# Scoring keys by queries in an attention and recurrence block, with row maxima from a product of their own, one head ahead

## The chip, the cores and the metric

The kernel runs on one core of a Trainium2 chip. The metric is device time in microseconds (us), the median of the runs. A core has five engines with queues of their own: PE (TensorE, matrix products), DVE (VectorE), ACT (ScalarE), POOL (GpSimd) and SP (SyncE, here it only issues transfers). They meet through semaphores: an instruction waits until a count is reached. PE reads its operands from SBUF (128 partitions) and writes to PSUM (8 banks of 512 fp32 columns). A product has a stationary operand, which is loaded first (PEld in the profile), and a moving one, which is streamed through.

## The reference

One transformer block on 1024 tokens of width 1024, fp32. An input projection feeds two mixers, which are joined by an output projection and followed by an MLP. The change lies in the first mixer:

```python
def block_fn(blk):                      # 128 queries of every head
    s = einsum(qb, kc) * scale          # 63 compressed keys
    p_cmp = masked_softmax(s, cmp_end <= t)
    o_cmp = einsum(p_cmp, vc)
    ...
    s = einsum(qb, k_sel) * scale       # 16 of 16 blocks: all keys up to t
    p = masked_softmax(s, pos <= t)
    o_slc = einsum(p, v_sel)
    ...
    s = einsum(qb, kwb) * scale         # the last 512 keys
    p = masked_softmax(s, wmask)
    o_win = einsum(p, vwb)
    return g0 * o_cmp + g1 * o_slc + g2 * o_win
```

There are 8 query heads of 64 dimensions and 2 groups of keys. As 16 blocks of 64 keys are all there are, the selection selects every block, and the second branch is plain causal attention.

## The kernel before

The stages follow one another: norm and transposes of the input, the projection in blocks of 512 columns (the compression of keys and values lies between two of them), the transposed keys, the attention of the first mixer, the recurrence of the second, the output projection, and the MLP. Each projection multiplies fp32 numbers as three products of a high and a low half (type fp32r).

The attention is a loop of four passages over two heads each. A passage has a list of 34 items. For a head there is one item for the compressed keys of all 1024 queries, and for each of the 8 tiles of 128 queries one over all keys so far ("slc", 1 to 8 key tiles) and one over the window ("win", 1 to 5 tiles): 66 key tiles in all, 36 and 30. Queries lie in PSUM partitions, keys along the columns. An item goes through these steps:

- PE (L1374) multiplies the stationary queries by the keys' high half and by their low half. `q_stack` holds the 64 dimensions twice, high half above, low half below, so that two products give nearly fp32. A product of identity and mask (L1379) adds the causal mask. An item has at least 256 columns and is cut in two banks over 512.
- DVE (L1058) takes the negative row maximum, and ACT (L835) writes exp(score − maximum) to `probs` with its row sum (an ACTIVATION_READ_ACCUMULATOR stands behind it).
- PE (L1389) transposes each 128x128 tile of `probs` into bank 4 or 5, and ACT (L849) or DVE (L1116) copies it to `probs_T`.
- PE (L1414) multiplies the stationary `probs_T` by the values (64 columns), in fp32: each such product stands in the trace as two MATMULs.
- DVE (L1087 to L1096) multiplies by the gates and the inverse sums and adds the result to `nsa`.

The compressed keys go the same way with a mask product (L1354), eight fp32 products of 64 columns (L1358), L1062, L1064, L826 and L1408. PE's order is written out by hand: transposes of item j, scores of item j+3, outputs of item j−1. The queries of the next heads are transposed at items 9 and 27 (L568; POOL copies them to `stage`, L665; ACT and DVE split them, L818, L1051). Ahead of the loop stand the same steps for the keys and for the first queries (L568, L805, L1035, L809, L1040), and behind it SP, POOL and ACT wait for the last output (`o_free`) before the recurrence begins.

## Time and profile before

| | |
|---|---|
| median of 3 runs | 1743.29 us (1740.09 to 1744.35) |
| profiled execution, first to last instruction | 1735.6 us |
| attention, from the transposes of the first queries to the last output | 364.2 to 698.2 us |
| PE busy over the whole span | 1573.1 us (91%) |
| DVE, ACT, POOL busy | 712.8 (41%), 443.6 (26%), 509.6 (29%) us |

Busy shares of PE are shares of recorded time: matrix products overlap in their records, so the step from one start to the next is the better measure of what one costs. The granted clock of TensorE is 1.0 where it runs at 2.4 GHz and 0.50 at 1.2 GHz.

### The profile page before, as it was taken

How to read it: one execution, taken by the hardware profiler on the slowest of the kernel's cores; microseconds unless marked ns; L12 is line 12 of the kernel's file. 1: busy time of each engine (PE TensorE's matmuls, PEld its weight loads, DVE VectorE, ACT ScalarE, POOL GpSimd, SP SyncE). 2: the span in 40 equal slices, each digit the busy share in tenths (PEclk: the TensorE clock that was granted, in tenths of full speed). 3: DMA queues.
4: the chain of work that ended last, by engine and by line, in shares of the span. 5: the costliest groups of instructions: out<-in, count | busy, mean ns of one | idle time of the engine just before them, and what ended most of it. 6: DMA issues, size and time to landing. Idle time of an engine off the chain costs nothing. (4 is left out here: it accounts for less than half of the span.)

```text
span 1735.6 us, 24765 instructions
## 1 busy us (share of the span) xinstructions
PE 1573.1 (91%) x8345; PEld 1328.8 (77%) x8345; DVE 712.8 (41%) x1311; ACT 443.6 (26%) x1007; POOL 509.6 (29%) x505
## 2 busy tenths in 40 slices
PE   3999999989999999467659989999999999999998
PEld 2988877878888888366548768888888888888886
DVE  5003830046576666899961143222222222222222
ACT  5014120144445455533361122020202020202020
POOL 1433322310000000665613313333333333333331
PEclk9999999979899999788979979999999999999999
DMA  4211131000000000100031101111111111111112
GB/s 143 62 48 49 37 97 32 17 6 2 0 0 0 0 0 0 45 0 0 0 121 46 60 16 49 49 48 48 47 48 44 48 48 48 48 48 43 53 43 97
DMA packets 36484, 69.09 MB, mean 40 GB/s; under 512 B 5688, under 2 KB 7264, under 8 KB 36448
## 3 DMA queue, kind: packets, MB, share of 16 engines
q1 hardware_dynamic: 34176, 67.78, 12.7%
q10 hardware_dynamic: 2272, 0.84, 0.2%
q8 instruction: 21, 0.34, 0.1%
q14 instruction: 15, 0.12, 0.0%
HBM read 64.41 MB, written 4.19 MB: 40 GB/s over the span
## 5 line engine op out<-in xcount | busy, mean ns | idle before, releaser
L427 POOL CAST w_high<-w_raw 128x512 fp32r<-128x512 f32 (+1 forms) x200 | 129.4, 647 | 767.8 <-issue 383.2
L429 POOL TENSOR_TENSOR w_low<-w_raw,w_high 128x512 fp32r<-128x512 f32 (+1 forms) x200 | 261.2, 1306 | 16.1
L435 PE MATMUL ps<-hT_high,w_high 128*128 128x512 f32 x640 | 249.8, 390 | 1.9 <-DVE hT_low L494 1.9
L435 PE MATMUL ps<-hT_low,w_high 128*128 128x512 f32 x640 | 249.5, 390 | 0.0
L435 PE MATMUL ps<-hT_high,w_low 128*128 128x512 f32 x640 | 249.4, 390 | 0.0
L1207 DVE TENSOR_TENSOR x<-ps,x 128x512 f32<-128x512 f32 x144 | 98.1, 692 | 285.8 <-PE ps L435 285.8
L435 PE MATMUL ps<-w_high,hidden_high 128*128 128x512 f32 x512 | 202.0, 394 | 2.0 <-ACT relu L932 1.9
L435 PE MATMUL ps<-w_high,hidden_low 128*128 128x512 f32 x512 | 199.4, 389 | 0.0
L435 PE MATMUL ps<-w_low,hidden_high 128*128 128x512 f32 x512 | 199.3, 389 | 0.0
L1240 DVE TENSOR_TENSOR relu_squared<-relu 128x512 f32<-128x512 f32 x64 | 57.1, 902 | 312.5 <-ACT relu L932 312.5
L932 ACT ACTIVATE relu<-ps 128x512 f32<-128x512 f32 x64 | 37.6, 588 | 574.4 <-PE ps L435 573.7
L435 PE MATMUL ps<-w_high,hT_high 128*128 128x512 f32 (+1 forms) x448 | 168.9, 377 | 4.1 <-DVE hT_low L494 3.1
L435 PE MATMUL ps<-w_low,hT_high 128*128 128x512 f32 (+1 forms) x448 | 168.8, 377 | 0.0
L435 PE MATMUL ps<-w_high,hT_low 128*128 128x512 f32 (+1 forms) x448 | 168.5, 376 | 0.0
L435 PEld LDWEIGHTS ps<-hT_high,w_high 128*128 128x128 f32 x640 | 120.5, 188 | 27.1 <-issue 2.1
L435 PEld LDWEIGHTS ps<-hT_high,w_low 128*128 128x128 f32 x640 | 120.5, 188 | 25.2
L435 PEld LDWEIGHTS ps<-hT_low,w_high 128*128 128x128 f32 x640 | 120.5, 188 | 25.1
L1414 PE MATMUL ps<-nsa,probs_T 128*128 x1056 | 138.3, 275 | 0.0
L1439 PE MATMUL ps<-hgrn_kq 128*128 128x128 f32 x448 | 77.3, 334 | 58.1 <-DVE hgrn_kq L1166 57.2
L1414 PEld LDWEIGHTS ps<-nsa,probs_T 128*128 128x128 f32 x1056 | 129.6, 194 | 0.0
L435 PEld LDWEIGHTS ps<-w_high,hidden_high 128*128 128x128 f32 x512 | 96.1, 188 | 31.2 <-ACT relu L932 8.9
L1439 PEld LDWEIGHTS ps<-hgrn_kq 128*128 128x128 f32 x448 | 68.5, 238 | 66.9 <-DVE hgrn_kq L1166 51.0
(179 smaller groups left out, 2356.3 us busy)
## 6 DMA issues: line engine op xcount, KB each, us to landing
w_raw<-in_w_mlp_in_dram SPq DMA_DIRECT2D x64, 256.0 KB, 2.7
w_raw<-in_w_mlp_out_dram SPq DMA_DIRECT2D x64, 256.0 KB, 2.7
w_raw<-in_w_in_dram SPq DMA_DIRECT2D x48, 256.0 KB, 2.7
x_in<-in_x_dram SPq DMA_DIRECT2D x8, 512.0 KB, 8.7
w_raw<-in_w_out_dram SPq DMA_DIRECT2D x16, 256.0 KB, 4.0
x<-in_x_dram SPq DMA_DIRECT2D x8, 512.0 KB, 7.6
out_dram<-x SPq DMA_DIRECT2D x8, 512.0 KB, 4.7
w_raw<-in_w_in_dram SPq DMA_DIRECT2D x8, 140.0 KB, 7.2
```

The costliest lines, as they stand in the source:

```text
L427: eng.tensor_copy(w_high[:, s, 0:width], w_raw[:, s, 0:width]).then_inc(w_highs, 1)
L429: eng.tensor_tensor(w_low[:, s, 0:width], w_raw[:, s, 0:width], w_high[:, s, 0:width].bitcast(F32), ALU.subtract).then_inc(w_split, 1)
L435: ins = nc.tensor.matmul(out_ap, a_hl[i], b_hl[j], start=first and n == 0, stop=last and n == 2)
L932: act.activation(relu[:, b % 4, :], ps[:, b, :], ACT.Relu).then_inc(m1_out, 1)
L1207: dve.tensor_tensor(xs, ps[:, t, :], xs, ALU.add).then_inc(res_out, 1)
L1240: dve.tensor_tensor(relu2[:, b % 4, :], relu[:, b % 4, :], relu[:, b % 4, :], ALU.mult).then_inc(sqd, 1)
L1414: ins = nc.tensor.matmul(ps[:, O_BANK + it.pair(j) % 2, c:c + DK], lhs, nsa[:, tiles[n], bass.ds(g * DK + v0, DK)], start=n == 0, stop=n = ...
L1439: ins = nc.tensor.matmul(ps[:, A_BANKS[u % len(A_BANKS)], h * P:(h + 1) * P], lhs(h), rhs(h), start=True, stop=True)
```

## The change

It leaves the stages around the attention as they are and writes the attention anew, without a loop over passages.

- Scores are made with keys in the partitions and queries in the columns (`scores_T`, L1330, L1331). The stationary operand is a tile of keys, the moving one up to 512 queries. The exponential of it is already `probs_T`, so the transposes of the probabilities and the copies of them are gone.
- The row maximum can't be subtracted by ACT's bias any more, since it runs along the columns. It becomes a further row of the contraction: the second key operand `k_low_and_ones` holds the low half of the keys in rows 0 to 63 and a row of ones at 64, 65 or 66 (one for each branch); the second query operand `q_and_max` holds the queries and, in these three rows, the negative maxima. It comes from a transpose of `q_max_stage`, in which POOL puts the queries and DVE the maxima.
- The maxima come from a product of their own (`scores_for_max`, L1299 to L1309), of the high half of the keys only, in the layout of before. There are 25 pieces of up to 512 columns for a head: one for the compressed keys and 24 of 1 to 4 key tiles. DVE takes the negative maximum of each (L1038, L1042) and joins those of queries 512 to 1023 from two parts (L1048). The pieces of head h+1 are made while head h is scored, two in each of the places 3 to 15.
- A head has 19 units of 512 columns (the last has 256), 6 for the first half of the queries and 13 for the second. In each place PE makes one unit's scores, then transposes or pieces for the next head, then the outputs of a unit two places back (up to four back at the start of a half, when outputs of three units come together in one place).
- The values get a column of ones (`v_and_ones`, 65 columns), so that the output product gives the row sums too; ACT's row sums are gone.
- The outputs of half a head fill two banks, and DVE empties them in four operations (`finalize`): reciprocal of 12 sums, times the gates, 768 products, and the sum of the three branches (L1057, L1059, L1063, L1067). The last two signal `o_free` and `y_done`.
- All compressed keys are fp32r now, as a high and a low half (`cmp_k_high`, `cmp_k_low_and_ones`); a key past the end takes the place of a masked row's sum, and the table `valid` is gone.

The core of the diff:

```diff
+EARLY = 9
+P_SLOTS = 6
+S_BANK, ST_BANK, T_BANK, O_BANK = 0, 2, 4, 6
+QT_AT, MAX_AT, Q2_AT = 0, 3, (9, 17)
...
+            def scores_for_max(h, c):
+                br, t, k0, k1, part = CHUNKS[c]
+                g, C = h // HPG, NM * h + c
+                if c == 0:
+                    pe.wait_ge(t_dve, q_low(h, 1))
+                if C >= 2:
+                    pe.wait_ge(max_done, C - 1)
...
+                ins = nc.tensor.matmul(o[:, 0:(k1 - k0) * P], QT[:, h % 2, t * P:(t + 1) * P], KS_H[:, br - 1, g, k0 * P:k1 * P],
+                                       start=True, stop=not tiles, skip_group_check=True)
...
+            def scores_T(h, u):
+                g, U = h // HPG, NU * h + u
+                if UNITS[u]["place"] == 0:
+                    pe.wait_ge(t_act, m_index(h, UNITS[u]["half"]) + 1)
+                if U >= 2:
+                    pe.wait_ge(exp_done, U - 1)
...
+                    nc.tensor.matmul(o, k1, QT[:, h % 2, qs], start=True, stop=False, skip_group_check=True)
+                    ins = nc.tensor.matmul(o, k2, Q2[:, h % 2, qs], start=False, stop=not tiles, skip_group_check=True)
...
+            for c in range(NM):
+                scores_for_max(0, c)
+            for half in range(2):
+                q_max(0, half)
...
+            for h in range(NH):
+                for u in range(NU):
+                    scores_T(h, u)
+                    if h + 1 < NH:
+                        if u in (QT_AT, QT_AT + 1):
+                            q_stack(h + 1, u - QT_AT)
+                        for c in range(2 * (u - MAX_AT), min(2 * (u - MAX_AT) + 2, NM)):
+                            if c >= 0:
+                                scores_for_max(h + 1, c)
+                        if u in Q2_AT:
+                            q_max(h + 1, Q2_AT.index(u))
+                    for h2, u2 in OUT_AT.get(NU * h + u, []):
+                        outputs(h2, u2)
```

And on DVE:

```diff
+            def finalize(h, half):
...
+                dve.wait_ge(pv_done, NU * h + [u for u, x in enumerate(UNITS) if x["half"] == half][-1] + 1)
+                o = out_view()
+                rec, cf = coef[:, 0, :, :], coef[:, 1, :, :]
+                at_.mark(dve.reciprocal(rec.rearrange("p (b t) r -> p b (t r)", b=2).unsqueeze(3), o[:, :, :, DK:OV]))
...
+            for h in range(NH):
+                for u in range(NU):
+                    if h + 1 < NH:
+                        if u in (QT_AT, QT_AT + 1):
+                            low_T(h + 1, u - QT_AT)
+                        for c in range(2 * (u - MAX_AT), min(2 * (u - MAX_AT) + 2, NM)):
+                            if c >= 0:
+                                maximum(h + 1, c)
+                    for h2, u2 in OUT_AT.get(NU * h + u, []):
+                        if UNITS[u2]["ends"]:
+                            finalize(h2, UNITS[u2]["half"])
```

How the instructions stand in a row shows it best at three places. First PE in the middle of a head. Before, an item of four key tiles: two transposes of the probabilities (of the item three back), two score products of 512 columns, a mask, two outputs.

```order
L1389 MATMUL ps<-eye,probs 128x128 [waits t_bank_emptied_by_act,exp_done]
L1389 MATMUL ps<-eye,probs 128x128
L1374 MATMUL ps<-k_high,q_stack 128x512
L1374 MATMUL ps<-k_low,q_stack 128x512
L1379 MATMUL ps<-masks 128x128
L1402 REGISTER_ALU
L1414 MATMUL ps<-nsa,probs_T 128x64 [waits t_bank_emptied_by_dve]
```

After, PE in places 8 and 9 of a head: the scores of a unit, two pieces for the maxima of the next head, again a unit and two pieces, and the transposes with the first half's maxima.

```order
L1330 MATMUL ps<-q_stack,k_high 128x512 [waits exp_done]
L1331 MATMUL ps<-q_and_max,k_low_and_ones 128x512
L1306 MATMUL ps<-k_high,q_stack 128x128 [waits max_done]
L1309 MATMUL ps<-masks 128x128
L1306 MATMUL ps<-k_high,q_stack 128x384 [waits max_done]
L1309 MATMUL ps<-masks 128x128
L1330 MATMUL ps<-q_stack,k_high 128x512 [waits exp_done]
L1331 MATMUL ps<-q_and_max,k_low_and_ones 128x512
L1306 MATMUL ps<-k_high,q_stack 128x256 [waits max_done]
L1309 MATMUL ps<-masks 128x128
L1306 MATMUL ps<-k_high,q_stack 128x512 [waits max_done]
L566 MATMUL ps<-eye,q_max_stage 128x128 [waits t_bank_emptied_by_dve,max_in_stage,q_max_stage_ready]
```

The transposes of the probabilities are gone, and every second product now waits for a maximum that DVE has taken two pieces earlier.

On DVE, before, in the middle of a passage: one maximum, one copy of transposed probabilities, and a short group for the outputs of one item alternate.

```order
L1058 TENSOR_REDUCE negmax<-ps 128x1 [waits qk_done]
L1113 REGISTER_ALU
L1116 COPY probs_T<-ps 128x512 [waits pv_done,t_full]
L1087 RECIPROCAL coef<-row_sums 128x2 [waits exp_done]
L105 REGISTER_ALU
L1089 ISA [waits att_step]
L1089 TENSOR_TENSOR coef<-coef,gates 128x2
```

After, DVE over one head: the compressed keys' maximum and nine more, the outputs of the first half of the queries, the fifteen other maxima, the joining of the parts, the low halves of the next queries, and the outputs of the second half.

```order
L1038 TENSOR_REDUCE q_max_stage<-ps 128x8 [waits t_full,scores_for_max_full]
L1042 TENSOR_REDUCE q_max_stage<-ps 128x1 [waits scores_for_max_full] x8
L1042 TENSOR_REDUCE part_max<-ps 128x1 [waits max_done,scores_for_max_full]
L1057 RECIPROCAL coef<-ps 128x12 [waits pv_done]
L1059 TENSOR_TENSOR coef<-coef,gates 128x12 [waits att_step]
L1063 TENSOR_TENSOR weighted_outputs<-ps,coef 128x768 [waits y_done,att_step]
L1067 TENSOR_REDUCE nsa<-weighted_outputs 128x4x64 [waits o_free]
L1042 TENSOR_REDUCE part_max<-ps 128x1 [waits scores_for_max_full] x15
L1048 TENSOR_TENSOR q_max_stage<-part_max 128x4x2 [waits max_done]
L1028 TENSOR_TENSOR q_stack<-ps,q_stack 64x512 [waits t_bank_emptied_by_act] x2
L1057 RECIPROCAL coef<-ps 128x12 [waits pv_done]
L1059 TENSOR_TENSOR coef<-coef,gates 128x12 [waits att_step]
```

The outputs now come in two long groups, and the maxima of pieces 10 to 24 stand behind the first of them.

Third, PE ahead of the first head. Before, the transposes of the first queries were followed by the scores of three items and then by the steady order. After, all 25 pieces of the first head come first (here the first and the last of them), then the transposes with the maxima, then the first unit.

```order
L1299 MATMUL ps<-cmask,masks 128x512 [waits t_bank_emptied_by_dve,cmp_k_low_ready,masks_loaded]
L1301 MATMUL ps<-cmp_k_high,q_stack 128x64 x8
L1306 MATMUL ps<-k_high,q_stack 128x128
L1309 MATMUL ps<-masks 128x128
```

```order
L1306 MATMUL ps<-k_high,q_stack 128x256 [waits max_done]
L1309 MATMUL ps<-masks 128x128
L566 MATMUL ps<-eye,q_max_stage 128x128 [waits t_bank_emptied_by_dve,max_in_stage,q_max_stage_ready]
L566 MATMUL ps<-eye,q_max_stage 128x128 x3
L566 MATMUL ps<-eye,q_max_stage 128x128 [waits t_bank_emptied_by_dve,max_in_stage,q_max_stage_ready]
L566 MATMUL ps<-eye,q_max_stage 128x128 x3
L1330 MATMUL ps<-q_stack,cmp_k_high 128x512 [waits v_and_ones_ready,t_bank_emptied_by_act,ones_rows_ready,t_bank_emptied_by_dve]
```

What moved is the whole maximum work of one head: it now lies between the first queries and the first unit.

## Rows read from the trace of the kernel before

**Rows 1.** The page: busy time of each engine (share) xinstructions, then 40 slices.

```profile
PE 1573.1 (91%) x8345; PEld 1328.8 (77%) x8345; DVE 712.8 (41%) x1311; ACT 443.6 (26%) x1007; POOL 509.6 (29%) x505
...
PE   3999999989999999467659989999999999999998
```

**Rows 2.** Windows over the attention: stretch, length, busy time of each engine, clock.

```profile
361.50:381.90 20.40, 17.08 (x76) 15.25 (x76) 8.44 (x17) 7.74 (x20) 2.29 (x3) 0.50 0.01 1
381.90:457.00 75.10, 71.23 (x587) 64.20 (x585) 50.80 (x123) 37.44 (x93) 2.03 (x2) 1.00 0.01 1
457.00:467.30 10.30, 9.89 (x44) 8.66 (x44) 4.57 (x12) 4.11 (x16) 0.00 (x0) 0.50 0.00 0
```

**Rows 3.** Windows over the second and the third passage of two heads.

```profile
457.40:541.30 83.90, 79.79 (x623) 72.15 (x623) 54.40 (x131) 40.96 (x106) 2.03 (x2) 0.94 0.00 0
541.30:621.50 80.20, 75.87 (x622) 68.21 (x622) 53.86 (x131) 40.77 (x105) 2.03 (x2) 1.00 0.00 0
```

**Rows 4.** PE's waits in the third passage: total us, times, longest.

```profile
PE ps L1389 <- DVE q_stack L1051: 2.0, 2, 1.0
PE ps L1389 <- ACT probs L826: 1.7, 1, 1.7
PE ps L1374 <- ACT probs L835: 0.6, 2, 0.4
```

**Rows 5.** Timeline of PE, third passage: start us, us, instruction (320-column products, outputs, transposes).

```profile
562.34 0.83 PE L1389 MATMUL ps<-eye,probs 128*128 128x128 f32 x6
562.92 0.39 PE L1374 MATMUL ps<-k_high,q_stack 128*128 x1
563.15 0.31 PE L1374 MATMUL ps<-k_low,q_stack 128*128 x1
563.30 0.23 PE L1379 MATMUL ps<-masks 128*128 128x128 bf16 x1
563.34 0.39 PE L1374 MATMUL ps<-k_high,q_stack 128*128 x1
563.57 0.31 PE L1374 MATMUL ps<-k_low,q_stack 128*128 x1
563.72 0.23 PE L1379 MATMUL ps<-masks 128*128 128x128 bf16 x1
563.79 1.28 PE L1414 MATMUL ps<-nsa,probs_T 128*128 x10
```

**Rows 6.** Timeline: products of 512 columns, the start of a passage (256 columns), and compressed keys.

```profile
585.90 0.40 PE L1374 MATMUL ps<-k_low,q_stack 128*128 x1
586.14 0.23 PE L1379 MATMUL ps<-masks 128*128 128x128 bf16 x1
...
616.99 0.38 PE L1354 MATMUL ps<-cmask,masks 128*128 128x512 bf16 x1
617.20 1.90 PE L1358 MATMUL ps<-cmp_k,q_stack 128*128 x16
...
622.12 0.28 PE L1374 MATMUL ps<-k_low,q_stack 128*128 x1
622.25 0.23 PE L1379 MATMUL ps<-masks 128*128 128x128 bf16 x1
```

**Rows 7.** Groups of the third passage: line, operation, count | busy us, mean ns.

```profile
L1058 DVE TENSOR_REDUCE negmax<-ps 128x1 f32<-128x512 f32 x4 | 2.6, 681 | 0.0
L1051 DVE TENSOR_TENSOR q_stack<-ps,q_stack 64x512 fp32r<-64x512 f32 x4 | 2.6, 691 | 4.2 <-ACT q_stack L818 4.2
L1058 DVE TENSOR_REDUCE negmax<-ps 128x1 f32<-128x384 f32 x4 | 2.2, 553 | 0.3 <-PE ps L1379 0.3
L818 ACT ACTIVATE q_stack<-ps 128x512 fp32r<-128x512 f32 x4 | 2.2, 595 | 1.3 <-PE ps L568 1.3
L1058 DVE TENSOR_REDUCE negmax<-ps 128x1 f32<-128x768 f32 x2 | 1.9, 953 | 0.0
L1058 DVE TENSOR_REDUCE negmax<-ps 128x1 f32<-128x256 f32 x4 | 1.7, 420 | 0.5 <-PE ps L1379 0.5
L1062 DVE TENSOR_REDUCE cmp_max<-ps 128x8 f32<-128x512 f32 x2 | 1.4, 692 | 1.4 <-PE ps L1358 1.4
L1058 DVE TENSOR_REDUCE negmax<-ps 128x1 f32<-128x128 f32 x4 | 1.1, 284 | 0.1
L1075 DVE RECIPROCAL cmp_max<-cmp_max 128x8 f32<-128x8 f32 x2 | 0.4, 193 | 0.0
```

**Rows 8.** Timeline of the start: the first queries, and PE's first products.

```profile
364.22 1.94 PE L568 MATMUL ps<-eye,stage 128*128 128x128 f32 x8 [0.65 <-DVE k_low L1035]
...
366.83 0.69 DVE L1040 TENSOR_TENSOR q_stack<-ps,q_stack 64x512 fp32r<-64x512 f32 x1 [0.16 <-ACT q_stack L809]
...
367.58 0.61 PE L1354 MATMUL ps<-cmask,masks 128*128 128x512 bf16 x1 [1.42 <-DVE q_stack L1040]
367.66 3.64 PEld L1358 LDWEIGHTS ps<-cmp_k,q_stack 128*128 128x128 f32 x16
367.98 3.52 PE L1358 MATMUL ps<-cmp_k,q_stack 128*128 x16
```

**Rows 9.** Timeline of the end: the last outputs on DVE, and ACT's next step.

```profile
697.60 0.28 DVE L1094 SCALAR_TENSOR_TENSOR nsa<-ps,coef,nsa 128x64 f32 x1 [2.42 <-PE ps L1414]
697.92 0.28 DVE L1096 SCALAR_TENSOR_TENSOR nsa<-ps,coef,nsa 128x64 f32 x1
...
698.24 3.90 ACT L861 ACTIVATE hgrn_logf<-hgrn_qf 128x1024 f32<-128x1024 f32 x4 [1.69 <-DVE nsa L1096]
```

**Rows 10.** Timeline of the step from the compressed keys to the projection that follows.

```profile
264.65 0.57 ACT L796 ACTIVATE cmp_v<-ps 64x128 f32<-64x128 f32 x2 [1.39 <-PE ps L1283]
```

**Rows 11.** A group of POOL over 500 to 1000 us: the costliest form of its kind.

```profile
L690 POOL TENSOR_SCALAR hgrn_k<-hgrn_qf 128x1024 f32<-128x1024 f32 x4 | 8.0, 2029 | 0.0
```

More of the change, by code:

```diff
@@ L193, with window, score_units @@
-PREP_AT = 9
-NEXT_AT = 27
-FIRST = 10
-PT_SLOTS = 10
-P_SLOTS = 4
-AHEAD = 3
-S_BANKS = 4
-T_BANK = 4
-O_BANK = 6
+CMP, SLC, WIN = 0, 1, 2
+def window(t):
+    return max(0, t - WIN_T), t + 1
+def score_units():
+    units = []
+    for half in range(2):
+        t0 = 4 * half
+        whole, parts = [], []
+        for br in (SLC, WIN):
+            for kt in range(t0 + 4):
+                qs = [t for t in range(t0, t0 + 4) if (kt <= t if br == SLC else window(t)[0] <= kt <= t)]
+                (whole if len(qs) == 4 else parts).append((br, kt, qs[0], len(qs)))
+        mine = [[(CMP, 0, t0, 4)]] + [[c] for c in whole]
+        while parts:
+            a = max(parts, key=lambda c: c[3])
+            parts.remove(a)
+            b = next((c for c in parts if c[3] + a[3] == 4), None)
+            if b:
+                parts.remove(b)
+            mine.append([a, b] if b else [a])
+        for place, chunks in enumerate(mine):
+            units.append(dict(half=half, place=place, chunks=chunks, ends=place == len(mine) - 1,
+                              width=sum(c[3] for c in chunks) * P))
+    return units
@@ L202, with out_slots @@
+OV = DK + 1
+def out_slots():
+    when = {}
+    for h in range(NH):
+        for u, unit in enumerate(UNITS):
+            at = NU * h + u + 2 + max(0, 2 - unit["place"])
+            when.setdefault(at, []).append((h, u))
+    return when
+OUT_AT = out_slots()
 D_SLOTS, E_SLOTS, X_SLOTS = 4, 3, 4
@@ L1123, in _, with low_T @@
[L1123 to L1127 removed]
+            at_ = Steps(att_step)
+            def low_T(h, half):
+                T = q_index(h, half)
+                dve.wait_ge(t_act, T + 1)
+                q = QT[DK:P, h % 2, half * BW:(half + 1) * BW]
+                dve.tensor_tensor(q, ps[DK:P, T_BANK + T % 2, :], q.bitcast(F32), ALU.subtract).then_inc(t_dve, 1)
@@ new lines, in _ @@
+            for half in range(2):
+                low_T(0, half)
+            for c in range(NM):
+                maximum(0, c)
+            for h in range(NH):
+                for u in range(NU):
[8 more added lines that the diff above has]
+                            finalize(h2, UNITS[u2]["half"])
@@ new lines, in outputs @@
+            def outputs(h, u):
+                g, U, unit = h // HPG, NU * h + u, UNITS[u]
+                if unit["place"] == 0:
+                    pe.wait_ge(o_free, 2 * h + unit["half"])
+                pe.wait_ge(exp_done, U + 1)
+                col = 0
+                for br, kt, q0, nq in unit["chunks"]:
+                    for q in range(q0, q0 + nq):
+                        tt = q - 4 * unit["half"]
+                        m = 3 * (tt % 2) + br
+                        v = V1c[:, g, :] if br == CMP else V1[:, br - 1, g, kt, :]
+                        ins = nc.tensor.matmul(ps[:, O_BANK + tt // 2, m * OV:(m + 1) * OV], PT[:, U % P_SLOTS, col:col + P], v,
+                                               start=br == CMP and tt % 2 == 0, stop=unit["ends"], skip_group_check=True)
+                        col += P
+                ins.then_inc(pv_done, 1)
@@ L1435, in _ @@
+            for at in sorted(OUT_AT):
+                if at >= NU * NH:
+                    for h2, u2 in OUT_AT[at]:
+                        outputs(h2, u2)
+            pe.wait_ge(o_free, 2 * NH)
             pe.wait_ge(bc_done, 4)
```

555 lines of the change are left out of this document (202 added, 353 removed).

## The prediction

> **What bounds the kernel now.** I read the page first: PE is busy 91% of the span, and its digit is 8 or 9 all through the attention (slices 9 to 16) [rows 1]. Then the windows over the attention: in a passage of two heads PE is busy 75.87 of 80.2 us, DVE 53.86, ACT 40.77, POOL 2.03 [rows 3]. So PE sets this stage, and what the change does to DVE and ACT counts only where PE waits for them. PE's waits in a passage are 2.0, 1.7 and 0.6 us [rows 4], 4.3 in 80.2. Last the clock. The stage begins at 0.50 and is at 1.00 from 381.9; a second stretch at 0.50 lies at 457.0 to 467.3, just behind the change from the first passage to the second, and makes that passage 83.9 instead of 80.2 us, 3.7 more [rows 2, 3]. From the transposes of the first queries at 364.2 to the last output at 698.2 the stage takes 334.0 us [rows 8, 9].
>
> **What a PE instruction costs.** The step from a start to the next, all at clock 1.00. A product of 320 columns 0.15 us (563.57 to 563.72) [rows 5], of 512 0.24, of 256 0.13 [rows 6], so 384 about 0.18 and 448 0.20. A mask 0.07 (563.72 to 563.79), and 0.05 more where an fp32r product follows it: product, product, mask, product's step is 0.42 (562.92 to 563.34) against 2 x 0.15 + 0.07 [rows 5]. Ten fp32 outputs take 1.28, the last one 0.275 of it in the pipeline: 0.112 each, two for a tile whatever its width. Six transposes in 0.83: 0.111 each [rows 5]. The wide mask 0.21 (616.99 to 617.20), and 16 for the compressed keys 0.112 each [rows 6].
>
> As a test, one head of before: products 20 x 0.15 + 8 x 0.13 + 8 x 0.18 + 4 x 0.20 + 8 x 0.24 = 8.2; masks 1.6; compressed scores 0.21 + 16 x 0.112 = 2.0; outputs 148 x 0.112 = 16.6; transposes (66 + 4 + 8) x 0.11 = 8.6. Sum 37.0. The trace has 40.1 for a head, of which 2.2 are the waits of rows 4 and 0.9 shorter ones.
>
> **One head after.** Removed: 70 transposes of probabilities, 7.7 us, and the fp32 compressed scores, 2.0. Unchanged: 148 outputs, 16.6. They have 65 columns instead of 64, and their step was the same 0.112 at 64 columns [rows 5] as a transpose of 128 has. Added or changed:
> - Products, both kinds together: 29 of 512 columns x 0.235, 17 of 384 x 0.18, 17 of 256 x 0.13, 13 of 128. The last are not in the trace; no fp32r product there has under 256 columns. Below they are bounded by one loading of weights, the 0.112 of an output's step, above by an fp32 product, two records, 0.224 [rows 5]. I take 0.112, since 256 columns at 0.13 are already close to it. Sum 6.8 + 3.1 + 2.2 + 1.5 = 13.5.
> - 40 masks x 0.07 and 30 x 0.05 behind them: 4.3 (before 1.6). Three wide masks 0.7. Eight short products on the compressed keys 0.9.
> - 16 transposes, 8 of the queries and 8 with the maxima: 1.8.
>
> Sum 37.7 us, 0.7 more than before. The transposes that go are paid back by the second pass over the scores (7.2 for the maxima: 4.2 of products, 1.9 of masks, 1.1 of compressed keys) and by masks that are now made twice.
>
> DVE and ACT get much less. DVE has for a head 25 reductions: 0.69 + 5 x 0.284, 0.42 and 0.553 by their widths, 0.681 for 512 [rows 7], 13.1 together, two low halves 1.4, and two groups of outputs; ACT 19 exponentials at about 0.6, as a 512-column copy from PSUM has 0.595 [rows 7], and four copies. That is about 20 and 14 us in 41, so neither becomes the bound by its sum.
>
> **Where PE waits after.** A group of outputs on DVE is a reciprocal 0.19, a product with gates about as much, 768 columns from PSUM about 0.95 (a reduction of 768 has 0.953), and a sum of 768, again 0.95 [rows 7]: with the gaps 2.6 us. Behind it stand the next maxima, and PE, in order, may be only two pieces ahead of them.
> - Places 7 to 9. The group starts 0.25 after the outputs of place 7. The maximum of piece 10 (0.284) is ready at 0.25 + 2.6 + 0.28 + 0.18 for the signal = 3.3. PE has up to piece 12 only two units and two pieces: 0.47 + 0.42 + 0.47 = 1.4. It waits 2.0 there, and 0.4 more at piece 13. Behind PE's wait stand the transposes with the maxima and the outputs of place 10.
> - Places 1 to 4. The low half of the next queries comes first: unit 1's exponential ends about 3.4 us into the head, ACT's copy takes 0.6, DVE 0.69 [rows 7], which makes 4.8. Then the group of the second half, 2.6, and the compressed keys' maximum, 0.69: ready at 8.2. PE gets to piece 2, which needs it, at 7.0. It waits 1.2, and 0.3 around it.
>
> Together 3.9 us for a head against the 3.1 of before. A head takes 41.6, before 40.1. Were DVE's group hidden, nothing else would be late: the exponentials are asked for two places later, about 4 us against 0.9.
>
> **The start.** All 25 maxima of the first head lie ahead of the first unit. The queries are ready 3.3 us after 364.2, as before [rows 8]. Then wide mask and eight products at clock 0.50, 0.43 + 8 x 0.22, with the handover 2.4; then the reductions. DVE needs 13.1, and PE at 0.50 as much for a piece as DVE (512 columns and mask 0.43 + 0.11 + 0.2 of loading, against 0.681), so that a part of the handovers shows: 17.8, between 13.1 and 25 x 0.74. Then the joining, four transposes and the signal: 1.0. First unit 24.5 us after 364.2. POOL's new work (ones rows, two operations of 2048 columns at twice the 2.03 of 1024 [rows 11], and values) ends about 12 us after 364.2 and is hidden under this; if the maxima took under 10 us it would show.
>
> **The end.** The last head makes no maxima and no queries: 37.7 − 7.2 − 1.8 = 28.7, and 0.9 of waits. Then a whole group of outputs, 2.7, where before DVE had two small operations left, 697.60 to 698.20 [rows 9].
>
> **The sum.** 24.5 + 7 x 41.6 + 29.6 + 2.7 = 348.0. I add one stretch at half clock as before, 3.7, since waits of this length stand at the passages' ends now too [rows 2, 3]: 351.7, against 334.0. Before, the slow clock at the start (to 381.9) fell on real work, about 8 us; now it falls on a time that DVE sets anyway, which is in the sum. The compression stage gives 0.3 back, one copy of 0.28 instead of two [rows 10]. Span 1735.6 + 17.7 − 0.3 = 1753; the median stands 7.7 above the profiled span, so **1761 us**, 1.0% slower.
>
> **The rivals.**
> - *Short products are dear.* If an fp32r product of 128 columns costs what an fp32 one does, 0.224, that is 13 x 0.112 and something at the 64-column ones, 1.5 to 1.9 us for a head. A part falls into waits that are there anyway, so I count 8 to 12 in all: 1771. For it: nothing in the trace runs below 256 columns in fp32r. Against it: the step at 256 shows no floor but the loading. The Trainium skill, FP8 and Floating Point Precision, section TensorE Precision Notes, says that true FP32 takes four passes and a reduced FP32 is read and truncated, with no word on a least width; by that the cheap case holds, and the trace agrees as far as its 256-column rows at 0.13 go.
> - *More half clock.* Each head now has a wait of 2.0 and one of 1.2. If a stretch like 457.0 to 467.3 came in every second head, three more would cost 11: 1772. For it: the one of before lies where two passages meet and PE waits [rows 2]. Against it: the third passage has a wait of 1.7 too and stays at 1.00 [rows 3, 4].
> - *Faster: PE never waits for the maxima.* The place is DVE's group in places 7 and 1. If it takes under 1.1 us, a third of what the rows give, piece 12 is never late. Then a head takes 37.7 to 38, 8 x 3.7 less, and with the clock steady 3.7 less again: 1761 − 30 − 4 = 1727. The rows of 0.69 for 512 columns speak against it.
> - *No difference.* Half of the waits hidden (slots filled in another way than I think) and no stretch at half clock: 1761 − 15 − 4 = 1742, within the bound.
>
> **How the numbers follow.** About 0.3% (5 us) is what a measurement of this kernel can tell from no change. Forecast 1761 with its own spread of 1750 to 1768: 0.45. Short products dear: 0.25. More half clock: 0.12, both slower. No difference: 0.10. Faster: 0.08. So slower 0.82, same 0.10, faster 0.08. The range leaves out the faster case and the ends where two slow cases meet: 1745 to 1779.
>
> **What would show each step.** PE's busy time in the attention stays about what it was and its outputs' step stays 0.112; in it DVE falls by about a quarter and ACT by a third. The first unit stands near 388.7. From a head's first unit to the next are 41 to 42 us, with two waits for maxima (L1306 on DVE L1042 and L1038) of 1 to 2.5 us each. L1331 at 128 columns shows a step of 0.11 or 0.22. I am wrong if a head takes under 40 us, if ones rows or values from POOL hold the first unit, or if ACT holds PE at every unit.

## The result, and the profile after

The changed kernel takes 1758.12 us, median of 4 runs (1751.31 to 1760.86), beside 1741.69 us for the kernel before in the same comparison (4 runs, 1737.9 to 1744.35). The ratio is 1.0084, with an interval of 1.0061 to 1.0106: slower by 16 us, and inside the range. Where single executions of a kernel below stand over 1.5% above its fastest, they are given apart and no comparison uses them.

| | before | after |
|---|---|---|
| profiled span, us | 1735.6 | 1749.5 |
| median of all runs in this comparison, us | 1741.69 | 1758.12 |
| attention, from 364.2 to DVE's last step on the outputs, us | 334.0 | 348.0 |
| first unit or score after 364.2, us | 3.4 | 23.4 |

The page of after, as [rows 1]: busy time of each engine (share) xinstructions, then 40 slices of TensorE (PE) and its granted clock.

```profile
PE 1582.6 (90%) x8160; PEld 1317.0 (75%) x8177; DVE 642.7 (37%) x1078; ACT 384.0 (22%) x774; POOL 521.2 (30%) x521
...
PE   3999999979999999466759969999999999999998
...
PEclk8999999979998999788879979999999999999999
```

DVE and ACT are relieved by 70 and 60 us, PE does 9.5 us more. The windows of after, as [rows 2, 3]: stretch, length, busy time of PE, PEld, DVE, ACT and POOL with the number of instructions, clock (the last two numbers are the transfers' share and rate). They are the start, the passage of the first head, that of the second, that of the fifth, and of the fifth again its first wait and the stretch at 0.50.

```profile
364.00:387.60 23.60, 19.39 (x69) 12.80 (x70) 14.59 (x29) 1.68 (x3) 8.37 (x10) 0.57 0.00 1
387.60:427.50 39.90, 37.74 (x279) 31.41 (x280) 16.16 (x32) 14.84 (x26) 2.27 (x3) 0.98 0.00 1
427.50:468.10 40.60, 38.15 (x291) 32.33 (x292) 18.46 (x36) 13.09 (x23) 1.66 (x2) 1.00 0.01 1
549.50:596.20 46.70, 45.75 (x291) 38.23 (x292) 18.64 (x36) 13.09 (x23) 1.66 (x2) 0.82 0.00 1
...
556.30:557.20 0.90, 0.18 (x2) 0.04 (x1) 0.90 (x3) 0.60 (x1) 0.00 (x0) 1.00 0.00 0
...
559.60:576.60 17.00, 16.93 (x65) 13.18 (x64) 6.65 (x12) 2.81 (x5) 0.00 (x0) 0.50 0.00 0
```

From a head's first unit to the next head's are 39.90, 40.65, 40.66, 40.65, 46.79, 42.24 and 40.65 us. At the full clock a head takes 40.65: 38.15 us of PE's work and two waits. The fifth takes 6.1 more, because 17.0 us of it run at 0.50; the sixth has 3.4 us at 0.50. PE's waits in the second head, as [rows 4]: total us, times, longest. Behind them the same two waits on PE's timeline, and the first of the two DVE groups that make them.

```profile
PE ps L1306 <- DVE part_max L1042: 1.6, 1, 1.6
PE ps L1306 <- DVE q_max_stage L1038: 0.8, 1, 0.8
```

```profile
434.28 0.23 PE L1336 MATMUL ps<-masks 128*128 128x128 bf16 x1
435.33 0.33 PE L1306 MATMUL ps<-k_high,q_stack 128*128 128x128 f32 x1 [0.81 <-DVE q_max_stage L1038]
...
446.15 0.40 PE L1331 MATMUL ps<-q_and_max,k_low_and_ones 128*128 128x512 f32 x1
448.12 0.39 PE L1306 MATMUL ps<-k_high,q_stack 128*128 128x256 f32 x1 [1.57 <-DVE part_max L1042]
```

```profile
432.18 0.23 DVE L1057 RECIPROCAL coef<-ps 128x12 f32<-128x12 f32 x1
432.44 0.17 DVE L1059 TENSOR_TENSOR coef<-coef,gates 128x12 f32<-128x12 f32 x1
432.65 0.96 DVE L1063 TENSOR_TENSOR weighted_outputs<-ps,coef 128x768 f32<-128x768 f32 x1
433.64 1.03 DVE L1067 TENSOR_REDUCE nsa<-weighted_outputs 128x256 f32<-128x768 f32 x1
434.59 0.68 DVE L1038 TENSOR_REDUCE q_max_stage<-ps 128x8 f32<-128x512 f32 x1
```

PE has written two pieces for the maximum and needs one of their banks back. DVE is in the group of outputs from 432.18 to about 434.6 and takes the compressed keys' maximum only then; PE goes on at 435.33. The second wait is the same with the other half: there DVE's group holds up the maximum of a later piece (L1042).

The end, as [rows 9]: a whole group of 2.5 us lies behind the last outputs.

```profile
709.75 0.23 DVE L1057 RECIPROCAL coef<-ps 128x12 f32<-128x12 f32 x1 [15.75 <-PE ps L1353]
710.02 0.17 DVE L1059 TENSOR_TENSOR coef<-coef,gates 128x12 f32<-128x12 f32 x1
710.22 0.96 DVE L1063 TENSOR_TENSOR weighted_outputs<-ps,coef 128x768 f32<-128x768 f32 x1
711.22 1.03 DVE L1067 TENSOR_REDUCE nsa<-weighted_outputs 128x256 f32<-128x768 f32 x1
```

So the account of the attention is: 23.4 start, 39.9 + 6 x 40.65 = 283.8 for seven heads at the full clock, 7.7 for the half clock, 30.6 for the last head, 2.5 for the end. That is 348.0, and 14.0 more than before: the difference of the two spans is 13.9.

### The profile page after: what moved, and what is told of

It is laid out like the page before. It is cut to its first block and busy times, and to the rows that moved or that the text cites. A ratio compares the mean times of both kernels' runs of the same rounds, so it can differ in the third digit from the quotient of the medians.

```text
span 1749.5 us, 22153 instructions
## 1 busy us (share of the span) xinstructions
PE 1582.6 (90%) x8160; PEld 1317.0 (75%) x8177; DVE 642.7 (37%) x1078; ACT 384.0 (22%) x774; POOL 521.2 (30%) x521
## 5 line engine op out<-in xcount | busy, mean ns | idle before, releaser
L423 PEld LDWEIGHTS ps<-hT_high,w_high 128*128 128x128 f32 x640 | 120.5, 188 | 27.3 <-issue 2.1
L1353 PE MATMUL ps<-v_and_ones,probs_T 128*128 128x65 f32 x1056 | 138.3, 277 | 0.1
L1353 PEld LDWEIGHTS ps<-v_and_ones,probs_T 128*128 128x128 f32 x1056 | 133.2, 197 | 1.0
L832 ACT ACTIVATE probs_T<-ps 128x512 f32<-128x512 f32 (+1 forms) x152 | 88.9, 586 | 199.9 <-PE ps L1336 148.3
```

The source lines that it names most:

```text
L423: ins = nc.tensor.matmul(out_ap, a_hl[i], b_hl[j], start=first and n == 0, stop=last and n == 2)
L832: act.activation(PT[:, U % P_SLOTS, 0:w], ps[:, ST_BANK + U % 2, 0:w], ACT.Exp).then_inc(exp_done, 1)
L1353: ins = nc.tensor.matmul(ps[:, O_BANK + tt // 2, m * OV:(m + 1) * OV], PT[:, U % P_SLOTS, col:col + P], v, start=br == CMP and tt % 2 == 0 ...
```

## The experiments

Twelve kernels were run. The first four were to confirm the reading of the waits and of the start, and all four came out slower than after, far from their theories.

### The sum of the branches made twice

```diff
+                at_.mark(dve.tensor_reduce(nsa[...], otmp[...], AX, ALU.add))
+                at_.wait(dve)
                 dve.tensor_reduce(nsa[...], otmp[...], AX, ALU.add).then_inc(y_done, 1)
```

> The changed kernel with the last operation of a group of outputs (the sum of three branches, 1.03 us) done twice, the first time with the same values. Theory (what stands ahead of the maxima on DVE is what PE waits for, one for one): both waits grow by 1.0 to 1.1 us, a head goes from 40.65 to 42.7, the stage grows by 15 us. Rival (the waits are the handover of the pieces, not the group): they stay at 1.6 and 0.8, a head at 40.7 to 41.

Measured: 1827.84 us (one run), 70 us slower than after. The first head has only one group in it, and a wait of 2.6 us instead of 1.57: one microsecond more on DVE is one microsecond more of wait, as expected. The other heads are 50.2 to 51.6 us long, one is 66.0. Windows of this kernel: the first head's passage, and the longest stretch at half clock.

```profile
390.10:432.50 42.40, 39.14 (x280) 32.36 (x279) 17.29 (x33) 14.94 (x26) 2.27 (x3) 0.95 0.00 1
442.00:496.60 54.60, 53.46 (x220) 44.84 (x218) 15.47 (x29) 8.36 (x14) 0.00 (x0) 0.50 0.00 1
```

The waits grew as the theory has it, and by it they are 15 us of the 70; what the kernel lost beyond them lies in heads with stretches at half clock.

### The groups later on DVE

The first half's group is taken one place later, the second's two, behind the next maxima in DVE's order.

```diff
-                    for h2, u2 in OUT_AT.get(NU * h + u, []):
-                        if UNITS[u2]["ends"]:
-                            finalize(h2, UNITS[u2]["half"])
+                    for h2, half in FIN_AT.get(NU * h + u, []):
+                        finalize(h2, half)
```

> The changed kernel with one thing moved: DVE does the outputs of the first half of a head behind the maxima of place 8 instead of place 7, and those of the second half behind the maxima of place 3 instead of in place 1. Theory (the two waits of PE for maxima, 1.6 and 0.8 us a head, are DVE's long group of outputs standing ahead of the maxima): both go, a head falls from 40.65 to 38.0 to 38.6 us, seven heads give 14 to 18 us, the span 1749.5 becomes about 1733 and the median about 1742. Rival (the maxima are late anyway, or the outputs' bank becomes the wait at places 4 and 10): the wait only moves to L1353 on DVE L1063, a head stays over 40 us and the span within 4 us.

Measured: 1803.87 us (1797.22 to 1813.82), ratio to before 1.0362 (1.0326 to 1.0399). Windows: one head undisturbed, then of the next its first part, its wait, and the stretch behind it.

```profile
441.40:482.20 40.80, 38.44 (x293) 32.48 (x292) 18.37 (x36) 13.09 (x23) 1.66 (x2) 1.00 0.01 1
482.20:489.70 7.50, 7.50 (x59) 6.11 (x57) 2.71 (x7) 3.77 (x7) 1.04 (x1) 1.00 0.00 0
489.70:490.70 1.00, 0.12 (x2) 0.10 (x1) 0.96 (x2) 0.20 (x1) 0.00 (x0) 0.99 0.00 0
490.70:511.20 20.50, 20.50 (x81) 17.05 (x82) 6.80 (x14) 2.95 (x5) 0.00 (x0) 0.50 0.00 1
```

PE's waits in that undisturbed head:

```profile
PE ps L1310 <- DVE part_max L1047: 1.3, 1, 1.3
PE ps L1357 <- DVE weighted_outputs L1068: 0.9, 1, 0.9
```

Two things are shown. The waits did not go. They moved: the outputs of the next half (L1357) now wait 0.9 us for DVE to free their two banks, the maximum waits 1.3 us one place later, and a head at the full clock takes 40.81 us, as much as in after. And in six of the seven passages the clock falls to 0.50 for 10 to 27 us, 113 us in all. Those six take 49.0 us more than six times 40.81. With the 3.3 us at 0.50 that the first of them still has of the start, a microsecond at half clock costs 0.42 here.

### The first unit earlier

The first unit comes behind nine of the first head's maxima; the sixteen others are spread over its units (a table replaces the fixed places). The diff's core:

```diff
-            for c in range(NM):
+            for c in range(EARLY):
                 scores_for_max(0, c)
-            for half in range(2):
-                q_max(0, half)
+            q_max(0, 0)
```

> The changed kernel with the first head's six units of the first half begun after 9 of its 25 maxima; the other 16 pieces stand between these units, and the next head's queries and pieces come in places 6 to 18. Theory (the start is 20 us of DVE's maxima with PE half idle): the first unit comes 11 to 12 us after the first queries are ready instead of 20.4, and the stage gets 6 to 10 us shorter, median about 1750. Rival (the start is held by the half clock, which lasts some 20 us whatever runs): the units now run at half clock, PE takes 14 us for what takes 7, and the stage gets at most 3 us shorter.

> Both edits together. Theory: the gains add, 20 to 26 us less than the changed kernel, median 1732 to 1738, faster than both kernels. Rival: they share a cause (PE's idle time at half clock), so together they give no more than the larger of them, median 1742 or above.

Measured: 1773.39 us, median of three runs (1761.66 to 1774.79; a fourth took 1806.27), ratio 1.0139 (1.0087 to 1.019). With both edits 1787.53 and 1798.75 us; two more runs took 1820.87 and 1823.8. The first unit does come 10.8 us earlier, at 376.8. But the first head then takes 71.6 us instead of 39.9. Its two parts:

```profile
376.80:404.60 27.80, 24.62 (x138) 18.13 (x138) 12.94 (x25) 8.80 (x15) 1.66 (x2) 0.81 0.00 1
404.60:448.40 43.80, 42.48 (x176) 35.30 (x175) 12.07 (x24) 6.36 (x11) 0.62 (x1) 0.50 0.00 0
```

PE is busy 42.48 us of the second part's 43.80, at 0.50. The step that the theories of all four expectations had in common was that the clock in the heads stays as it was.

### Does a wait bring the clock down?

I laid the granted clock beside PE's timeline for before, after and these four kernels. From the first unit to the last output it falls 27 times, and each fall starts 1.0 to 4.3 us behind the beginning of a wait of PE of 0.8 us or more (the shortest 0.77): 457.0 in before behind the 1.7 us wait at 455.7 [rows 2]; 559.6 in after behind that of 0.81 at 556.5, and 617.6 behind that of 1.57 at 615.3; 490.7 above behind that of 0.88 at 489.7. Not every such wait is followed by one: after has twelve of them and 2 falls. Standing near is not causing. The test is to fill the waits with work that is of no use: if waits cause the falls, the kernel gets faster with it.

```diff
+            def filler(h, n):
+                for _ in range(n):
+                    nc.tensor.matmul(ps[:, T_BANK + 1, :], KS_H[:, 0, 0, 0:P], QT[:, h % 2, 0:BW], start=True, stop=True,
+                                     skip_group_check=True)
...
+                        filler(h, FILL.get(u, 0))
                         for c in range(2 * (u - MAX_AT), min(2 * (u - MAX_AT) + 2, NM)):
```

> The kernel with the groups one and two places later, and in each head but the last eight extra fp32r products of 512 columns (0.24 us each, results unused) into a free transpose bank, just ahead of its two waits of TensorE: 3 ahead of the wait of 0.88 us for o_free, 5 ahead of the wait of 1.33 us for a maximum. So TensorE works there where it waited, and has 56 products more to do. Theory (each fall of the granted clock in the attention starts 0.9 to 3.7 us behind such a wait, and is caused by it): the half-clock stretches of the heads go (123 us between 388 and 703 before this edit), each head takes about 40.8 us as its one undisturbed head did, and the time comes down from 1803.9 to 1744-1752 us although work is added. Rival (the clock falls because TensorE is kept too busy, or by the hour, and the waits only stand near): the falls stay or grow, 1804 us or more.

> The changed kernel with the same filling ahead of its own two waits in each head but the last: 3 products ahead of the 0.81 us wait (place 4), 6 ahead of the 1.57 us wait (place 9). Theory (the waits bring the clock down): no half-clock stretch between 389 and 700 us, heads of 40.65 us each, span 1742-1744 us, median 1744-1750 instead of 1758. Rival (waits do not matter to the clock): 1758 us or a little over.

By the clock's rows the half clock of the first of the two kernels between 388 and 703, before this edit, is 116 us (113 in six falls, and 3.3 left of the start), not 123.

Measured: the kernel with the groups later falls from 1803.87 to 1748.61 us (1747.51 to 1750.17, ratio 1.0038, 1.0025 to 1.005), 55 us less with 56 products more. After falls from 1758.12 to 1746.97 us (1743.41 to 1752.58, ratio 1.003, 1.0017 to 1.0043), 11 us less with 63 more. The timeline of the first of them: three filling products (L1349) stand where the wait of 0.88 was. Then its window from the first unit to the last output, and that of the filled after from its second head on.

```profile
439.07 0.93 PE L1349 MATMUL ps<-q_stack,k_high 128*128 128x512 f32 x3
440.14 1.10 PE L1364 MATMUL ps<-cmp_v_and_ones,probs_T 128*128 128x65 f32 x8
```

```profile
391.20:707.00 315.80, 311.85 (x2316) 262.17 (x2315) 131.25 (x256) 105.78 (x184) 8.89 (x11) 1.00 0.00 1
```

```profile
430.90:705.00 274.10, 272.30 (x2034) 229.76 (x2034) 115.61 (x224) 90.91 (x158) 6.63 (x8) 1.00 0.00 1
```

The clock is at 1.00 from 391.9 us in the first and from 392.2 in the second; from the second head on, heads take 40.80 to 40.82 us in the first and 40.64 to 40.67 in the second, and no fall is left in either. The waits cause the falls. A cause in too much work for PE is out, since the filled kernels have more of it. No run puts the same products away from the waits, so these two alone leave open that more work anywhere would do; the kernel of the next section has no such products, only shorter waits, and no fall either.

Which wait is followed by a fall seems to go with where the waits lie in time. From its second head on the kernel with the early start has the waits of after, and there the clock has come back 38.6 us ahead of that head, as in after. The same sequence follows in both: 170.7 us at 1.00, 17.1 at 0.50, 41.0 at 1.00 and 3.4 at 0.50. Two traces show the likeness; the reason was not found.

### Shorter groups

With that, the waits are worth more than their length, and the question is what takes them away rather than moves them. The sum is the one step of a group that reads SBUF alone, so it can go to POOL, which has 1.66 us of work in a head. (The Trainium skill, GPSIMD Engine Reference, section Engine selection, has POOL without a port to PSUM and about twice as slow as DVE in elementwise work of two inputs; the steps of the group that read PSUM stayed on DVE, and no run here shows POOL beside PSUM. The two additions of 256 columns take POOL 0.73 and 0.72 us below; no run has the same addition on DVE.)

```diff
-                dve.wait_ge(o_free, n + 1)
-                dve.tensor_reduce(nsa[...], otmp[...], AX, ALU.add).then_inc(y_done, 1)
+            def branch_sum(h, half):
+                n = 2 * h + half
+                y = nsa[:, 4 * half:4 * half + 4, h * DK:(h + 1) * DK]
+                pool.wait_ge(o_free, n + 1)
+                pool.tensor_tensor(y, otmp[:, :, 0, :], otmp[:, :, 1, :], ALU.add).then_inc(y_part, 1)
+                pool.wait_ge(y_part, n + 1)
+                pool.tensor_tensor(y, y, otmp[:, :, 2, :], ALU.add).then_inc(y_done, 1)
```

> The changed kernel with the last step of each DVE group (the sum of the three branches, 1.03 us on DVE) made on GpSimd as two additions of 256 columns; DVE's group is 1.36 us instead of 2.39. Theory (TensorE waits for maxima that stand behind the group): the wait of 0.81 us goes, that of 1.57 us comes down to about 0.6, a head takes about 38.9 us at the full clock instead of 40.65, 12 us over seven heads, and the falls of the clock become rarer: 1738-1748 us. Rival (the wait goes to another place, as it did where the groups stood later): heads stay at 40.6 and the time within 4 us of 1758.

Measured: 1733.81 us (1730.61 to 1736.7), ratio 0.9955 (0.9937 to 0.9972): 24 us faster than after, and 0.5% faster than before. DVE and POOL behind the outputs of the second half of the head before, and the window from the second head to the last output:

```profile
431.66 0.96 DVE L1078 TENSOR_TENSOR weighted_outputs<-ps,coef 128x768 f32<-128x768 f32 x1
432.58 0.69 DVE L1053 TENSOR_REDUCE q_max_stage<-ps 128x8 f32<-128x512 f32 x1
...
432.70 0.73 POOL L698 TENSOR_TENSOR nsa<-weighted_outputs 128x256 f32<-128x256 f32 x1 [7.43 <-DVE weighted_outputs L1078]
433.51 0.72 POOL L700 TENSOR_TENSOR nsa<-nsa,weighted_outputs 128x256 f32<-128x256 f32 x1
```

```profile
426.50:688.00 261.50, 258.25 (x1979) 220.09 (x1979) 101.47 (x210) 90.82 (x158) 26.82 (x36) 1.00 0.00 1
```

The maximum now follows the multiplication at once; POOL's 1.45 us lie beside it. A head takes 38.57 us, 2.08 less; one wait of 0.5 us is left in it. No fall of the clock is left. Of the 24 us, 13.5 are from shorter heads (1.07 in the first, 2.08 in each of six) and the rest from the clock, which cost 7.7 us in the profiled run of after and more in its median, as the filled kernel shows with its 11.

### The early start once more

> The kernel with the sum on GpSimd, and the first head's start changed as in the kernel with early units: the first unit comes behind nine of head 0's 25 maxima instead of behind all, the other sixteen are made between its units, and those of head 1 later in the same passage. Theory: the first unit comes 10.8 us earlier (near 377), the passage of head 0 takes about 5 us more of second-pass products and DVE's maxima, and, if it has no wait of 0.8 us or more any longer, it runs at the full clock: 38.8 + 5 to 7 us, so the time is 1728-1731 against 1733.8 us. Rival (head 0's passage is bound by DVE, which has both heads' maxima in it, TensorE waits, and the clock falls as it did for 47.8 us in the kernel with early units alone): 1740-1755 us.

Measured: 1742.05 us (1736.15 to 1746.24), ratio 0.9996 (0.9978 to 1.0013): 8 us slower than without the early start. The number is the rival's, the reason is not. The first head's passage, in two parts:

```profile
378.30:408.20 29.90, 28.24 (x106) 21.80 (x108) 9.06 (x18) 6.75 (x11) 0.62 (x1) 0.50 0.00 1
408.20:438.00 29.80, 27.69 (x207) 22.88 (x206) 14.61 (x30) 8.65 (x15) 3.06 (x4) 1.00 0.00 1
```

DVE is busy 9.06 of 29.90 us and 14.61 of 29.80, so it does not bind. The clock has been at 0.50 since 367.2 and stays there until 408.2, while PE is busy 28.24 us of the 29.90. The first unit comes at 378.3, 9.4 us earlier than without the early start (387.7), but this head takes 59.7 us instead of 38.8. Of these 20.8 us, 5 to 7 were expected for the added work; of the other 14 to 16, the 29.9 us at half clock are about 12.6 (an estimate, at the 0.42 found above). In after the half clock of the start (368.4 to 388.9) lies on the first head's maxima, in which PE and DVE wait for one another in turn; what it costs there no run shows.

How long the half clock of a start lasts is open. It came back 20.5 to 34.1 us after its fall in the kernels that make all the first maxima ahead of the first unit, and after 27.3, 41.0 and 41.0 us in the three with the early start. In the first part above PE has waits of 0.2 to 0.5 us at five places; whether they hold the clock down was not tested.

### What the parts of a head cost

The first of these kernels is after without the products for the maxima and without DVE's reductions; the second is the one with the sum on POOL without the masks in these products. Both compute something else: the exponential's scale is 0. A line of each:

```diff
             def scores_for_max(h, c):
-
+                return
...
@@ the second kernel
-                tiles = [(kt, 1 if kt == t else 2) for kt in range(k0, k1) if kt == t or (br == WIN and kt == t - WIN_T)]
+                tiles = []
```

> The changed kernel without the second product and all maxima (the exponential's scale is 0, so nothing overflows): what remains is the first pass, the q stacks, the exponentials, the outputs and the groups. Theory (the second pass costs TensorE 7.2 us a head and the DVE waits of 2.4 us, and the start 17.8 us): a head takes 30.5 us, with no wait over 0.5 us, and the time is about 1755 - 8 x 10 - 17 = 1655-1665 us. Rival (another limit is close below, ACT's exponentials or the order): heads of 35 us or more, 1690 us or more.

> The kernel with the sum on GpSimd, without the 20 masks of 128 columns in the second product of each head (the maxima are then taken over keys of the future too; the exponential's scale is 0, so nothing overflows). The sum put the 40 masks of a head at 4.3 us, those of the second pass at 1.9. Theory (TensorE's work sets the length): a head goes from 38.57 to 36.5-36.9 us at the full clock. Rival (the products reach DVE's maxima sooner and wait there instead): 38.0 us or more.

Measured: without the maxima 1664.89 us (one run), heads of 30.73 us, the first unit at 373.4. With 38.57 − 0.5 = 38.1 us of work in the whole head and a wait of 0.25 in the 30.73, the second product costs PE 7.6 us; the sum had 7.2. The first unit waits 3.7 us for POOL's values here, which end at 373.4, 9.2 us after 364.2; the prediction had 12. Without the masks in it 1720.17 us (one run), heads of 36.79 us: 1.78 less at the full clock, where the sum had 1.9; the wait left in a head grows from 0.50 to 0.63. Windows of one head in each:

```profile
404.50:435.30 30.80, 30.54 (x241) 26.92 (x240) 6.19 (x10) 12.87 (x23) 1.66 (x2) 1.00 0.00 1
```

```profile
461.80:498.60 36.80, 36.02 (x272) 31.57 (x273) 16.45 (x34) 13.11 (x23) 4.52 (x6) 1.00 0.00 1
```

Of what the change adds, the maxima are by far the largest part: 93 us of 1758 hang on them, the start and the clock included.

### The outputs rounded to fp32r, in both kernels

The outputs are the largest part of a head, 148 records at 0.112 us. Exponentials and values are rounded to fp32r for this product (with a 66th column in the values of the changed kernel), which leaves one record where fp32 has two: once on the kernel with the sum on POOL (its main lines follow) and once on the kernel before.

```diff
-    V1 = sb("v_and_ones", [P, 2, NG, NT, OV], F32, 49152)
-    PT = sb("probs_T", [P, P_SLOTS, BW], F32, 65536)
+    V1 = sb("v_and_ones", [P, 2, NG, NT, OV], F32R, 49152)
+    PT = sb("probs_T", [P, P_SLOTS, BW], F32R, 65536)
```

> [...] Theory (TensorE's work sets the length of a head now): 74 records of 0.112 us fewer in each of the 8 heads, 8.3 us, 66 us in all, head 30.3 us and 1664-1672 us. Rival (DVE's 17 us and ACT's exponentials with their latency show as waits, and the clock falls with them): 1680 us or more.

> The kernel before, with its transposed exponentials and its values rounded to fp32r for the product with the values (the same rounding as in the kernel with the sum on GpSimd and fp32r outputs; the values are rounded in place by GpSimd). Question: is the gain of that rounding open to the kernel before as well, or only to the changed order? Theory A (a head of before is TensorE's work, 37.0 us, and 16.6 of it are outputs, so half of them, 8.3, go): 66 us less, about 1676 us. Theory B (with 27 us of DVE and 20 us of ACT in a head, and each output behind exponential, transposes and a copy, part of the 8.3 us comes back as waits, and the clock falls at them): a head is 33-36 us and the time is 1690-1715 us.

Measured: 1670.24 us (2 runs, 1669.73 to 1670.75), ratio 0.9593 (0.9553 to 0.9632), with the sum on POOL; 1691.86 us (4 runs, 1688.42 to 1695.98), ratio 0.9724 (0.9696 to 0.9753), for the kernel before. Both kernels compute the whole, with exponentials and values rounded to fp32r. One head of the first at the full clock, and four heads of the second:

```profile
451.90:482.80 30.90, 30.03 (x217) 24.17 (x218) 16.40 (x34) 13.07 (x24) 4.50 (x6) 1.00 0.00 1
```

```profile
439.70:579.80 140.10, 127.84 (x945) 110.52 (x948) 106.18 (x261) 82.17 (x208) 4.05 (x4) 0.95 0.00 0
```

PE's waits in those four heads of the kernel before. In four heads with fp32 outputs (455.6 to 619.8) the first two lines were the same, the third was not there, and the fourth was 1.0 us.

```profile
PE ps L1393 <- DVE q_stack L1055: 3.9, 4, 1.0
PE ps L1393 <- ACT probs L830: 3.4, 2, 1.7
PE ps L1378 <- DVE nsa L1085: 2.1, 2, 1.0
PE ps L1378 <- ACT probs L839: 1.3, 2, 0.9
```

With the changed order and the sum on POOL a head loses 7.65 of its possible 8.3 us. Before, it loses 5 (40.1 at the full clock to 35.0 here). Of the 13 us that are missing in these four heads, PE's longer waits for finishing steps on DVE and exponentials on ACT are 2.4, and 13.6 us at half clock are about 5 at the price found above; the rest, some 5 us, is not accounted for. The clock falls five times between 443 and 624. Over the whole kernel the rounding takes off 64 us with the changed order and 50 before. So the change alone costs 16 us, but with the sum on POOL it leaves DVE and ACT with so little that a cut in PE's work arrives almost in full. No run has the rounding on after itself.

The Trainium skill, FP8 and Floating Point Precision, section TensorE Precision Notes, gives true FP32 four passes, and says of the reduced form that it is read and truncated. The traces here show two records for each of 74 fp32 products of 65 columns and one for each fp32r product of 66, at nearly the same step of 0.112 us. So the price is two to one at this width, where the page's four passes would let one expect more; the measurement decides.

## Why the prediction came out right, point by point

- **PE's work in a head.** 37.7 us were summed; 38.15 are there. The bound with the widest ends, fp32r products of 128 columns, fell at the low end: the step from L1331 of 128 columns to its mask is 0.12 us, not 0.22, and that of one of 256 columns is 0.12 too. The rival of dear short products is out. The second product measured 7.6 (summed 7.2), its masks 1.8 (1.9). The steps of 128 and of 256 columns:

```profile
432.15 0.28 PE L1331 MATMUL ps<-q_and_max,k_low_and_ones 128*128 128x128 f32 x1
432.27 0.23 PE L1336 MATMUL ps<-masks 128*128 128x128 bf16 x1
...
438.67 0.28 PE L1331 MATMUL ps<-q_and_max,k_low_and_ones 128*128 128x256 f32 x1
438.79 0.23 PE L1336 MATMUL ps<-masks 128*128 128x128 bf16 x1
```

- **The waits.** Their place and their cause were right: two in each head, on L1306, for L1042 and L1038 behind DVE's groups. Their size was too large: 1.57 and 0.81 us, where 2.4 and 1.5 were summed. The group itself takes 2.4 us, not 2.6, and PE reaches the first wait at 434.5, 7.0 us into the head as summed, but finds the compressed keys' maximum 0.8 us on, at 7.8 instead of 8.2. So a head takes 40.65 us instead of 41.6, 7 us over all.
- **The start.** 23.4 us where 24.5 were summed; POOL's new work did not show, and its copies of the values end at 371.8, 7.6 us after 364.2 where 12 were put. That DVE sets this time was only in part right: from 368.4 to 387.6, at half clock, PE is busy 16.67 us and DVE 12.61. The end 2.5 for 2.7, the last head 30.6 for 29.6.
- **The clock.** One stretch was allowed for, 3.7 us. The profiled run has 7.7 us, and the median of after stands 6.8 above that run; filling the waits takes 11.2 us off the median. This step was sized too low. In the profiled run the terms without the clock come to 340.3 us where 348.0 were forecast, and the clock to 7.7 instead of 3.7: the forecast of 1761 against 1758 owes some of its closeness to two errors of opposite sign. The rival of more half clock gave the argument against it that a wait of 1.7 us need not bring a fall. That holds, and after shows it too (12 waits, 2 falls); but the mechanism was doubted with it, and the filled kernels show it to be real.
- **The faster rival.** It asked for a group under 1.1 us (two fifths of the 2.6 in the sum, not a third as it says) and gave 1727. With the group at 1.36 us the wait is nearly gone, the clock stays up, and the time is 1734: the mechanism holds, but the changed kernel has the group of 2.4 us that the rows of before told of.

What stays open: why the groups taken later, with waits of 0.88 and 1.33 us in a head where after has 0.81 and 1.57, bring the clock down in six of seven passages and after's own in two. Also open is how long the clock stays down once it has fallen: 3.4 to 54.6 us were seen.

## What to carry to other kernels

An engine that waits for a queue of small steps behind one long group on another engine was helped here by a shorter group, not by another place for it: moved, one of the two waits came back at the next shared buffer, and the other a place later. On TensorE a wait of about one microsecond in the middle of dense work can cost more than its length (two falls behind twelve such waits cost 7.7 us in after), and a cheap test of that is to fill it with products nobody reads. And a change that takes work off engines which do not bind can lose alone and still, once its own waits are short, be the better ground for the next cut on the one that does.

## What the hardware showed that was not expected

- Adding 56 products of 512 columns, 13 us of PE's work, where PE waited 0.88 and 1.33 us made a kernel 55 us faster: the granted clock, at 0.50 (1.2 GHz) for 113 us in six of its passages, is then 1.00 (2.4 GHz) from 0.8 us behind the first unit to the last output.
- Such a fall starts 1.0 to 4.3 us behind the beginning of a wait of 0.8 us or more and lasts 3.4 to 54.6 us although PE is busy all through it (20.50 of 20.50 us in the window at 490.7). In six kernels no wait over 0.64 us stands between the first unit and the last output (both filled ones, the sum on POOL, that without masks, that without maxima, and the sum on POOL with fp32r outputs), and there is no fall in them. A longer wait need not bring one: after has 12 of them and 2 falls.
- A microsecond of the attention at 0.50 costs 0.42 us (groups later) and 0.36 us (fifth head of after, 6.1 for 17.0), less than half in part because PE's waits shrink in it: the wait that is 1.57 us elsewhere in after is 0.07 in its fifth head (576.14 to 576.21).
- An fp32r product of 128 columns steps in 0.12 us, as one of 256 does.
